# Two joined transformer blocks on one core: norm factors applied to the products, attention transposed one item later, and some waits made finer

## What is computed

```python
mem_n = rms_norm(mem, ln_mem)
for layer in range(2):
    h = rms_norm(x, ln_mix[layer])
    mkv = mem_n @ w_mem_kv[layer]                       # keys and values of the memory
    if layer == 0:  mix_out, mem_q = gated_deltanet_mixer(h, ...)
    else:
        proj = h @ swa_w_q[0]                           # "swaq"
        q = apply_partial_rope(proj[..., :768], cos, sin)
        mix_out = sliding_window_attention(q, shared_k, shared_v, sinks); mem_q = proj[..., 768:]
    mem_o = memory_attention(mem_q, mem_k, mem_v)
    x = x + concat([mix_out, mem_o]) @ w_out[layer]      # "wout0", "wout1"
    x = x + swiglu(rms_norm(x, ln_ffn[layer]), w_gate_up[layer], w_down[layer])   # "gu", "dn"
    if layer == 0:
        kv = rms_norm(x, ln_kv) @ w_kv                  # "kv"
        shared_k, shared_v = apply_partial_rope(kv[..., :128], cos, sin), kv[..., 128:]
x = rms_norm(x, ln_final)
h = rms_norm(x, pre_norm_mix) * (1 + scale_m) + shift_m  # second block: "qlat", "misc", "zed", ...
...                                                     # sparse attention, a state-space mixer, another swiglu
```

## Time and profile before

| | |
|---|---|
| median of 3 runs | 2893.23 us |
| the profiled execution: time, span | 2904.37 us, 2902.6 us |
| PE busy | 2674.2 us, 92% of the span |
| DVE, ACT, POOL busy | 1542.4, 1039.7, 1017.5 us |
| mean granted clock of PE | 0.96 of full speed |

### The profile page before, as it was taken

How to read it: one execution, slowest core, us unless ns; L and a number is a source line. 1 busy time by engine, 2 the same in 40 slices (tenths; PEclk the granted TensorE clock), 3 DMA queues, 4 the chain that set the end, 5 groups by cost and what they waited for, 6 DMA issues and landing times.

```text
span 2902.6 us, 35230 instructions
## 1 busy us (share of the span) xinstructions
PE 2674.2 (92%) x13600; PEld 2024.7 (70%) x13600; DVE 1542.4 (53%) x2049; ACT 1039.7 (36%) x1569; POOL 1017.5 (35%) x264
## 2 busy tenths in 40 slices
PE   5999878999988788999979999899999998799996
PEld 4677836888867466888857776585445886588885
DVE  2745654442446745433255278897553676644244
ACT  3544443322232533222233344443443452332221
POOL 3335723344442013434423432332001553244442
PEclk9999979999999899999989999999999999899998
DMA  4224511222231012222223333334332332122321
GB/s 170 67 82 157 192 59 58 101 89 100 101 107 58 15 39 78 89 99 88 100 86 113 116 109 109 109 116 139 88 109 95 119 114 87 58 91 97 102 87 72
DMA packets 59807, 280.50 MB, mean 97 GB/s; under 512 B 9859, under 2 KB 11357, under 8 KB 32419
## 3 DMA queue, kind: packets, MB, share of 16 engines
q1 hardware_dynamic: 47155, 259.72, 26.7%
q10 hardware_dynamic: 12528, 19.06, 1.8%
HBM read 259.28 MB, written 19.40 MB: 96 GB/s over the span
## 4 chain that ended last, share of the span: by engine, by line
PE 43%; issue 37%; DVE 8%; POOL 8%; DMA 2%; ACT 2%; POOLq 0%; ACTq 0%; SPq 0%; DVEq 0%
PE banks L516 8%; PE banks L518 8%; PE banks L517 8%; POOL w_lo L2655 7%; DVE cs L1973 2%; PE banks L2043 2%; PE banks L2025 2%; DMA spill<-cs 2%; PE banks L2033 2%; DVE tmp L1867 1%; PE banks L1311 1%; PE banks L2154 1%; PE banks L2153 1%; PE banks L2152 1%; PE banks L2052 1%
## 5 line engine op out<-in xcount | busy, mean ns | idle before, releaser
L2655 POOL TENSOR_TENSOR w_lo<-raw,w_hi 128x2048 fp32r<-128x2048 f32 x176 | 814.5, 4628 | 1497.7 <-ACT w_hi L495 1432.8
L516 PE MATMUL banks<-hn_hi,w_hi 128*128 128x512 f32 (+1 forms) x2072 | 823.6, 397 | 69.6 <-DVE hn_lo L584 39.1
L517 PE MATMUL banks<-hn_lo,w_hi 128*128 128x512 f32 (+1 forms) x2072 | 819.8, 396 | 0.0
L518 PE MATMUL banks<-hn_hi,w_lo 128*128 128x512 f32 (+1 forms) x2072 | 818.6, 395 | 0.0
L495 ACT ACTIVATE w_hi<-raw 128x2048 fp32r<-128x2048 f32 x182 | 348.8, 1916 | 616.6 <-PE banks L518 586.3
L516 PEld LDWEIGHTS banks<-hn_hi,w_hi 128*128 128x128 f32 x2072 | 395.8, 191 | 183.6 <-issue 72.5
L517 PEld LDWEIGHTS banks<-hn_lo,w_hi 128*128 128x128 f32 x2072 | 396.1, 191 | 85.8 <-issue 0.5
L518 PEld LDWEIGHTS banks<-hn_hi,w_lo 128*128 128x128 f32 x2072 | 395.4, 191 | 85.6
L700 DVE TENSOR_TENSOR hid_lo<-prod,hid_hi 128x512 f32 x66 | 301.6, 4570 | 125.8 <-ACT hid_hi L673 125.8
L517 PE MATMUL banks<-hid_lo,w_hi 128*128 128x512 f32 x528 | 208.3, 394 | 0.0
L518 PE MATMUL banks<-hid_hi,w_lo 128*128 128x512 f32 x528 | 207.6, 393 | 0.0
(11 more groups left out here) (454 smaller groups left out, 3642.8 us busy)
## 6 DMA issues: line engine op xcount, KB each, us to landing
raw<-in_W SPq DMA_DIRECT2D x202, 1024.0 KB, 4.9
spill<-cs ACTq DMA_DIRECT2D x64, 256.0 KB, 4.0
oh<-codes SPq DMA_DIRECT2D x128, 128.0 KB, 2.7
extra<-in_W SPq DMA_DIRECT2D x8, 1024.0 KB, 4.9
grp<-spill SPq DMA_DIRECT2D x8, 512.0 KB, 4.5
grp<-spill SPq DMA_DIRECT2D x16, 256.0 KB, 4.9
zt<-spill SPq DMA_DIRECT2D x8, 512.0 KB, 3.6
x<-in_xT SPq DMA_DIRECT2D x1, 2048.0 KB, 14.3
```

The lines of the kernel that those rows point to most:

```text
L516: pe.matmul(out, wh, xh(k), start=(k == 0), stop=False)
L517: pe.matmul(out, wh, xl(k), start=False, stop=False)
L518: mm = pe.matmul(out, wl, xh(k), start=False, stop=(k == nkt - 1))
L2655: pool.tensor_tensor(w_lo[:, u % 2, :], raw[:, u % 2, :], w_hi[:, u % 2, :].bitcast(F32), ALU.subtract).then_inc(S("w_lo"), 1)
```

## The change

The norm's factor is the same for all features of a position, so it can be applied to a product instead of to its input. The change does so in four places, and changes five others.

- After wout0 and wout1: ACT and DVE split x * gain (without rs) as soon as each tile of x is there (`early_parts`; in place of the normed tiles, in the second half of hid_hi and hid_lo). The first two gate/up units (four output tiles) run on these. `pe_squares` moves from ahead of the first unit into it, ahead of its k tile 3. DVE multiplies the four products by rs at their evacuation, ACT applies Silu in SBUF. From the third unit on the normed tiles are used, which are made meanwhile; the third unit waits for them tile by tile.
- After dn02: kv runs on x * gain; its keys are multiplied by rs, its values (positions on partitions) by a column of factors kvr, for which PE sums the squares once more (`pe_rstd_col`). Norm 3's tiles are not made. Norm 4's tiles go to buffers of their own (nt, t_hi, t_lo), ahead of dve_kv and of the rotary tables on DVE.
- After dn12: norms 6 and 7 are made into one factor, from the squares of x * gain and of x (`pe_both_squares`). Norm 6 is written into x later, after `dve_small`.
- PE waits before each item of attention 1 for its own query tile and the key only. The rotations of tiles 4 and 5 stand in attention 1's first two items on DVE.
- In attention 1 the transposes come three items after the scores and the values four (TURN), with four buffers pr in place of three.
- ACT rounds wout0's second unit after attention 0, not in it.
- ACT loads the table of Sqrt by a small Sqrt at the start of `act_squares`.
- Two more constants are set by POOL at the start.

```diff
+ROPE_LATE = (4, 5)
+TURN = (2, 3)
...
-    k.rotate([("rope", j) for j in (6, 0, 1, 2, 3, 4, 5)], [4, 5, 6, 7])
+    k.rotate([("rope", j) for j in (6, 0, 1, 2, 3, 4, 5)], [4, 5, 6, 7, 4, 6, 7])
...
-    pr = sb("pr", [P, 3, 2, 256], F32, s2)
+    pr = sb("pr", [P, 4, 2, 256], F32, s2)
...
+NORMED = {0: 0, 1: 1, 2: 2, 4: 3, 5: 4}
+EARLY = {"wout0": 0, "dn02": 1, "wout1": 2}
+EARLY_GAIN = {"wout0": 2, "dn02": 3, "wout1": 5}
...
+def early_parts(name):
+    return (hn_hi, hn_lo) if name == "dn02" else (hid_hi[:, 1], hid_lo[:, 1])
...
+def norm_parts(i):
+    return (lambda k: nt[:, k % 4, :], t_hi, t_lo) if i == 4 else (lambda k: tmp[:, k, :], hn_hi, hn_lo)
...
+def early_ready(pe, name, key, extra=None):
+    def ready(k):
+        if k == 3:
+            pe_squares(pe, name, key, sq_tmp)
+            if extra:
+                extra()
+        pe.wait_ge(S("early_lo"), KT * EARLY[name] + k + 1)
+    return ready
...
 def act_squares(a, name, key, src, sq):
+    a.activation(root_of_eps[:, :], eps[:, :], ACT.Sqrt).then_inc(S("root_table"), 1)
+            if name in EARLY:
+                g = EARLY_GAIN[name]
+                a.activation(early_parts(name)[0][:, k, :], src(k), ACT.Copy, scale=gains[:, g, k:k + 1])\
+                    .then_inc(S("early_hi"), 1)
+            if name == "dn12":
+                a.activation(sq2[:, k, :], src(k), ACT.Square, scale=gains[:, 6, k:k + 1])\
+                    .then_inc(S("gain_squared"), 1)
+    if name == "dn12":
+        full(a, ("norm", 7))
+        a.activation(rs[:, :], bank(("norm", 7))[:, :], ACT.Sqrt, bias=eps2[:, 0:1], scale=1.0 / D)\
+            .then_inc(reads(("norm", 7)), 1)
-    a.activation(rs[:, :], bank(key)[:, :], ACT.Sqrt, bias=eps[:, 0:1], scale=1.0 / D)\
-        .then_inc(reads(key), 1)
+    a.activation((rs6 if name == "dn12" else rs)[:, :], bank(key)[:, :], ACT.Sqrt, bias=eps[:, 0:1],
+                 scale=1.0 / D).then_inc(reads(key), 1)
+    if name == "dn02":
+        full(a, key)
+        a.activation(kvr[:, :], bank(key)[:, 0:NC], ACT.Sqrt, bias=eps[:, 0:1], scale=1.0 / D)\
+            .then_inc(reads(key), 1)
...
+        if name in EARLY:
+            hi, lo = early_parts(name)
+            g = EARLY_GAIN[name]
+            v.wait_ge(S("early_hi"), KT * EARLY[name] + k + 1)
+            v.scalar_tensor_tensor(out=lo[:, k, :], in0=x[:, k, :], scalar=gains[:, g, k:k + 1],
+                                   in1=hi[:, k, :].bitcast(F32), op0=ALU.mult, op1=ALU.subtract)\
+                .then_inc(S("early_lo"), 1)
...
+def pe_both_squares(pe):
+    one, two = ("norm", 6), ("norm", 7)
+    pe.wait_ge(S("gain_square_added"), KT - 2)
+    pe.matmul(bank(two)[:, :], ones[:, :], sq2[:, 0, :], start=True, stop=False)
+    pe.wait_ge(S("square_added"), 6 * r + 6)
+    pe.matmul(bank(two)[:, :], epsm[:, :], tmp[:, 0, :], start=False, stop=False)
+    pe.matmul(bank(one)[:, :], ones[:, :], tmp[:, 0, :], start=True, stop=False)
+    pe.wait_ge(S("gain_squared"), KT)
+    pe.matmul(bank(two)[:, :], ones[:, :], sq2[:, KT - 1, :], start=False, stop=False)
+    pe.wait_ge(S("tile_squared"), KT * r + KT)
+    pe.matmul(bank(two)[:, :], epsm[:, :], tmp[:, KT - 1, :], start=False, stop=True).then_inc(fills(two), 1)
+    pe.matmul(bank(one)[:, :], ones[:, :], tmp[:, KT - 1, :], start=False, stop=True).then_inc(fills(one), 1)
...
+def pe_rstd_col(pe):
+    for b in range(NC):
+        bb = slice(b * P, (b + 1) * P)
+        for m in (0, KT - 1):
+            mm = pe.matmul(bank(key)[:, b:b + 1], tmp[:, m, bb], ones[:, 0:1], start=(m == 0), stop=(m > 0))
...
 def pe_ffn(pe, f, ready):
-        pe_linear(pe, name, ready=ready if c == 0 else None)
+        if f == 2 or c:
+            return pe_linear(pe, name, ready=ready if c == 0 else None)
+        early = (lambda k: hid_hi[:, 1, k, :], lambda k: hid_lo[:, 1, k, :])
+        unit_jobs(pe, U[name, 0], 0, *early, KT, ready=early_ready(pe, f"wout{f}", ("norm", 2 + 3 * f)))
+        unit_jobs(pe, U[name, 1], 0, *early, KT)
+        unit_jobs(pe, U[name, 2], 0, *hn_of, KT, ready=ready)
+        unit_jobs(pe, U[name, 3], 0, *hn_of, KT)
+        over_units(pe, name, lambda u, i: unit_jobs(pe, u, i, *hn_of, KT), 4)
...
+def act_early_gate(a, f, n):
+    u = U[f"gu{f}0", n]
+    prep_hi(a, u)
+    taken(a, ("unit", u, 0))
+    a.activation(sg[:, n, :], sg[:, n, :], ACT.Silu).then_inc(S("early_silu"), 1)
...
+def act_early_hidden(a, f, n):
+    a.wait_ge(S("early_prod"), 2 * f + n + 1)
+    a.activation(hid_hi[:, 0, n, :], prod[:, n, :], ACT.Copy).then_inc(S("hid_hi"), 1)
...
+def dve_early_scaled(v, f, n):
+    for t, dst in ((0, sg), (1, prod)):
+        key = ("unit", U[f"gu{f}0", n], t)
+        full(v, key)
+        v.tensor_tensor(dst[:, n, :], bank(key)[:, :], rs[:, :], ALU.mult).then_inc(reads(key), 1)
...
+def dve_early_hidden(v, f, n):
+    v.wait_ge(S("early_silu"), 2 * f + n + 1)
+    taken(v, ("unit", U[f"gu{f}0", n], 1))
+    v.tensor_tensor(prod[:, n, :], prod[:, n, :], sg[:, n, :], ALU.mult).then_inc(S("early_prod"), 1)
+    v.wait_ge(S("early_prod"), 2 * f + n + 1)
+    v.wait_ge(S("hid_hi"), FT * f + n + 1)
+    v.tensor_tensor(hid_lo[:, 0, n, :], prod[:, n, :], hid_hi[:, 0, n, :].bitcast(F32), ALU.subtract)\
+        .then_inc(S("hid_lo"), 1)
...
+            first = 2
+            act_early_hidden(a, f, 0)
+            act_early_gate(a, f, 1)
+            act_early_hidden(a, f, 1)
...
+            dve_early_hidden(v, f, 0)
+            dve_early_scaled(v, f, 1)
+            dve_early_hidden(v, f, 1)
...
-    for u in (AFTER, AFTER + 1):
-        a.wait_ge(w_land[u % 2], (u // 2 + 1 - FEWER) * 16)
-        a.activation(w_hi[:, u % 2, :], raw[:, u % 2, :], ACT.Copy).then_inc(S("w_hi"), 1)
...
+        if layer == 1 and n < len(ROPE_LATE):
+            taken(v, ("unit", U["swaq", ROPE_LATE[n] // 2], ROPE_LATE[n] % 2))
+            dve_rope(v, ROPE_LATE[n])
...
+    ready = early_ready(pe, "dn02", ("norm", 3), lambda: pe_rstd_col(pe))
-        hn_ready(pe, 3)(k)
+        ready(k)
...
-    v.tensor_copy(qraw[:, 6, :], bank(("unit", u, 0))[:, :]).then_inc(reads(("unit", u, 0)), 1)
+    v.tensor_tensor(qraw[:, 6, :], bank(("unit", u, 0))[:, :], rs[:, :], ALU.mult)\
+        .then_inc(reads(("unit", u, 0)), 1)
-    v.tensor_copy(vs[:, :, :], chunked(bank(("unit", u, 1))[:, :])).then_inc(reads(("unit", u, 1)), 1)
+    v.tensor_tensor(vs[:, :, :], chunked(bank(("unit", u, 1))[:, :]),
+                    kvr[:, :, None].broadcast_to([P, NC, P]), ALU.mult).then_inc(reads(("unit", u, 1)), 1)
...
+    if j == 6:
+        pe.wait_ge(S("land_rope"), 16 * ROPE_LOADS)
...
+def dve_first_block_out(v):
+    taken(v, ("norm", 6))
+    v.reciprocal(rs6[:, :], rs6[:, :]).then_inc(S("out_rstd"), 1)
+    v.wait_ge(S("out_rstd"), 1)
+    for k in range(KT):
+        v.scalar_tensor_tensor(out=x[:, k, :], in0=x[:, k, :], scalar=gains[:, 6, k:k + 1],
+                               in1=rs6[:, :], op0=ALU.mult, op1=ALU.mult).then_inc(S("first_out"), 1)
...
-        v.scalar_tensor_tensor(out=tmp[:, k, :], in0=x[:, k, :], scalar=gain2[:, 2 * idx, k:k + 1],
+        v.scalar_tensor_tensor(out=tmp[:, k, :], in0=x[:, k, :], scalar=gain[:, k:k + 1],
...
+    v.tensor_tensor(gg[:, :], gains[:, 6, :], gain2[:, 0, :], ALU.mult).then_inc(S("modulated"), 1)
...
     act_recurrence(a)
+    act_output_hi(a, AFTER + 1)
-    act_norm_round(a, 2)
+    act_norm_round(a, 2, between=lambda: act_early_gate(a, 0, 0))
...
-    act_norm_round(a, 3)
+    act_norm_round(a, 4)
+    prep_hi(a, U["kv", 0])
+    prep_hi(a, U["swaq", 0])
     rope_tables_act(a)
-    prep_hi(a, U["kv", 0])
-    act_norm_round(a, 4)
-    over_units(a, "swaq", lambda u, i: prep_hi(a, u, i))
+    for i in range(1, 4):
+        prep_hi(a, U["swaq", i])
...
-    act_norm(a, 7, x_of, T, lambda e, k: e.wait_ge(S("final"), k + 1))
...
-    dve_norm(v, 2, 2, x_of)
+    dve_norm(v, 2, 2, x_of, between=lambda: dve_early_scaled(v, 0, 0))
...
-    dve_norm(v, 3, 3, x_of)
+    taken(v, ("rstd_col",))
+    v.reciprocal(kvr[:, :], kvr[:, :]).then_inc(S("kv_rstd"), 1)
+    dve_norm(v, 4, 4, x_of)
+    v.wait_ge(S("kv_rstd"), 1)
+    dve_kv(v)
     rope_tables_dve(v)
-    dve_kv(v)
-    dve_norm(v, 4, 4, x_of)
     for i in range(4):
...
-            taken(v, ("unit", U["swaq", j // 2], j % 2) if j < 6 else ("unit", U["kv", 0], 0))
-            dve_rope(v, j)
+            if j not in ROPE_LATE:
+                taken(v, ("unit", U["swaq", j // 2], j % 2) if j < 6 else ("unit", U["kv", 0], 0))
+                dve_rope(v, j)
...
-    dve_rstd(v, 6, T, 5)
-    for k in range(KT):
-        v.scalar_tensor_tensor(out=x[:, k, :], in0=x[:, k, :], scalar=gains[:, 6, k:k + 1],
-                               in1=rs[:, :], op0=ALU.mult, op1=ALU.mult).then_inc(S("final"), 1)
     dve_modulation(v)
     dve_small(v)
+    dve_first_block_out(v)
...
-    pe_squares(pe, "wout0", ("norm", 2), sq_tmp)
     pe_ffn(pe, 0, hn_ready(pe, 2))
-    pe_squares(pe, "dn02", ("norm", 3), sq_tmp)
```

(44 more changed lines are left out.)

93 lines of the change are left out of this document (64 added, 29 removed).

## The result

The kernel after takes 2860.66 us (median of 4 runs, 2859.35 to 2868.89) against 2893.19 before (4 runs): a ratio of 0.9883, 95% interval 0.986 to 0.9905. That is faster by 32.5 us, half of the 65.5 forecast, and outside the range. Yet nearly all the steps of the sum came out close to what was worked out. What is missing was lost in a place that the sum put at nothing: in the long stretches without pauses the 128x512 matmuls come 1.9% further apart.

A forecast was written before the change was run, and what follows sets the result against it. PE, busy 2674.2 of 2902.6 us, bounds the kernel. 11.7 + 11.7 + 3.7 + 21 + 3 + 14.4 = 65.5 us off profiled 2904.37, less an 11.1 offset, gives 2828 us; range 2811 to 2850.

The forecast's parts named there:

- at nothing: Sqrt's table load, POOL's constants at the start and DVE's multiplications at the evacuation: no separate gain or cost.
- fourth rival: Matmul pace in the FFNs, 0.229 or 0.233 us: each FFN moves 6.8 us, 2821 or 2835; no chance of its own.
- rival on the pace: The fourth rival by another name: both FFNs at 0.229 or both at 0.233 us a matmul.
- wout0 to FFN 0: Pause behind the norm before FFN 0 goes, since unit 0 starts once tile 0 is split: 11.7 us gained.
- wout1 to FFN 1: Same code and same pause of 8.32 us before FFN 1: 11.7 us gained.
- first rival: Weights late in the gates, or attention's entry late: 9 to 23 us lost, 2837 to 2851, say 2843; chance 0.2.
- The weight split: Before wout0, POOL splits the second unit later, so PE starts earlier: 3.7 us gained, between 0 and 4.7.
- dn02 to the attention: From dn02's end through kv and swaq to attention 1's third item's exponentials: 21 us gained, bounds 14 and 26.
- The transposes: Attention 1's transposes an item later, against PE's wait for divided probabilities: 3 us gained, between -1 and 12.
- second rival: Deeper attention 1 removes all PE waits for transposes: 12 to 15.8 us in place of 3, about 2817; chance 0.15.
- dn12 to qlat: Two norms made into one factor between dn12's end and qlat's first product: 14.4 us gained, bounds 10 and 16.
- third rival: DVE's added two-input operations held by POOL on PE's path, 4.6 us each: 20 give 2920, 30 give 2966; chance 0.04.

The follow-up runs named there:

- second profile of before: The kernel before, profiled once more with no edit: 2890.40 us (one run).
- after_unshifted: Kernel after with its five small tiles declared above everything else, nearly all other tiles at their addresses of before: 2835.02 us, ratio 0.979 against the kernel before.
- before_moved_64: Kernel before with one unused tile of 64 bytes declared behind eps: 2919.47 us (one run).
- before_moved_2048: Kernel before with one unused tile of 2048 bytes declared behind eps: 2899.47 us (one run).

## Why the prediction was wrong

- **The step that failed is "at nothing"**, with the fourth rival. Of the added constants I weighed only POOL's writes; that they and three other tiles are declared ahead of the activations, and move every one that a matmul reads by 640 bytes, I did not look at. The rival on the pace saw the two values, 0.229 and 0.233, but priced two FFNs at 6.8 us each and put both signs inside the forecast's range. The price of a unit was right (11.20 less 10.99), but the pace changed in the units of the whole program, some 130, and in one direction: 27.5 us, shown by the unused tiles, and given back by the old addresses. The range's upper end, 2850, was made of late weights and left the pace out.
- **wout0 to FFN 0 and wout1 to FFN 1** were right: 11.5 (115.1 less 103.6) and 11.9 (103.4 of the second profile of before, less 91.5) for 11.7. No unit waited for weights; the first rival did not come.
- **The weight split** was right: 4.1 for 3.7.
- **dn02 to the attention** was right: 20.7 for 21, the loss in the first items included. PE enters the attention 71.3 us behind dn02, for "about 69".
- **The transposes** were nearly right: 3.1 to 4.3 for 3, at the same granted clock. The stage gained 5.7 in the profiles of the table, but some 2 of it came with the higher clock of that execution, which the prediction did not have: luck. The second rival was right on the wait and wrong on the time: it moved to the values.
- **dn12 to qlat** was right: 13.8 for 14.4.
- **The third rival**, held splits, was cut off the path at wout0 and wout1, as argued. In dn02 and dn12, whose units are 2.7 us shorter, it decided (the second profile of before against after_unshifted): 1.8 us each, 3.6 in all, where I had written 0.
- **The sum** of the stages in after_unshifted is 4.1 + 11.5 + 20.7 + 5.7 + 11.9 + 13.8 - 3.6 = 64.1 for 65.5; its measured gain is 63.2. That it comes so near is in part chance: the transposes' clock gave some 2 us and the tails took 3.6. Of the offset of 11.1 between profile and median, 5.5 was FFN 1's slow pace (291.2 less 285.7); what remains lies in stages that differ from one execution to the next.

What stays open: by what the address sets the pace, and why one stage alone had another pace in three executions (FFN 1 of before and of before_moved_64, wout0 of before_moved_2048). The weights' own addresses were not varied, nor any address of a single tile.

## What to carry to other kernels

When a change declares new tiles, compare the addresses of the old ones before and after, and put new small tiles behind everything the matmuls read; an edit that is worth nothing can cost 1% of the time through them. Compare the matmul interval in a stage without pauses first (count per window, clock 1.00) and only then the waits. A deferred step is not worth the wait that it removes from PE (15.4 us here, for some 4): look where the wait stands afterwards, and compare such a stage only between executions with the same granted clock.

## What the runs showed of the hardware

With the granted clock at 1.00 and no gap, 128x512 matmuls come at 0.229, 0.232, 0.233 or 0.234 us, by where the activations lie: the same program was 27.5 us slower with them 640 bytes higher, 2919.47 against 2897.54 us (one run against a median) with 64 bytes, and within the spread of its runs with 1024 or 2048 (2901.14 and 2899.47, one run each). A DVE split with two SBUF operands takes 0.75 us free, 3.84 when it meets POOL's split of 4.59 in dn02, and 4.57 in the kernel before; one held split in each unit of dn02, with ACT's rounding and POOL's next split behind it, is enough to let the units come 9.5 us apart instead of 8.4.
